# Strassen's scheme in the first projection and in the gate chunks of a two-block transformer kernel

## The reference, cut to what matters

```python
xn = rmsnorm(h, g_mix)                       # 256 x 2048
(q_a, k_c, v_c, k_s, v_s, k_w, v_w, g_nsa, c_q, c_kv, k_r,
 gate_a, gate_b) = jnp.split(xn @ w_in, bounds, axis=-1)
# q_a 1536 columns, then k_c, v_c, k_s, ... to k_r; gate_a and gate_b 2048 columns each
o_a = nsa_attention(...)                     # compressed, selected and window branches
o_b = mla_attention(...)
mixed = (sigmoid(gate_a) * (o_a @ w_o_nsa) + sigmoid(gate_b) * (o_b @ w_o_mla))
h = h + mixed @ w_out
```

## Time and profile before

| | |
|---|---|
| median of 3 runs | 2749.98 us (2749.94 to 2750.15) |
| the profiled execution: its time | 2749.45 us |
| its span | 2747.7 us |
| TensorE's mean granted clock | 0.998 |
| busy: TensorE, its weight loads, VectorE, ScalarE | 99%, 83%, 69%, 51% |
| matmuls | 12990 |
| HBM | 504.08 MB read, 184 GB/s |

### The profile page before, as it was taken

One profiled execution on the slowest core, in us unless ns is written; L12 is line 12 of the kernel. 1 busy time (PEld: TensorE's weight loads), 2 busy tenths in 40 slices (PEclk: granted clock), 3 DMA queues, 4 the chain that ended last, 5 costly groups with the idle time before them and its releaser, 6 DMA issues.

```text
span 2747.7 us, 30993 instructions
## 1 busy us (share of the span) xinstructions
PE 2732.1 (99%) x12990; PEld 2269.7 (83%) x12990; DVE 1882.3 (69%) x1699; ACT 1404.9 (51%) x1532; POOL 14.8 (1%) x28
## 2 busy tenths in 40 slices
PE   9999999999999999999999999999999999999999
PEld 7888778888888888888888888888788888888887
DVE  5445765455468878878788685665888489659765
ACT  5435663345566556455465545354554355445553
POOL 0000000000000000000000000000000000000000
PEclk9999999999999999999999999999999999999999
DMA  7645036555545555555555654545566555655555
GB/s 237 222 148 169 32 107 200 199 184 199 174 164 205 193 199 181 202 198 192 207 186 182 227 198 145 178 162 196 194 207 206 184 197 193 207 184 199 188 181 171
DMA packets 225082, 508.18 MB, mean 185 GB/s; under 512 B 9570, under 2 KB 20400, under 8 KB 224048
## 3 DMA queue, kind: packets, MB, share of 16 engines
q1 hardware_dynamic: 222752, 495.62, 52.8%
q0 software_dynamic: 2016, 10.36, 1.2%
q10 hardware_dynamic: 176, 0.23, 0.1%
HBM read 504.08 MB, written 2.10 MB: 184 GB/s over the span
## 4 chain that ended last, share of the span: by engine, by line
PE 86%; DVE 1%; ACT 1%; DMA 0%; issue 0%; ACTq 0%
PE acc L855 13%; PE acc L856 13%; PE acc L860 13%; PE acc L1338 7%; PE acc L1343 7%; PE acc L1339 7%; PE tb L1343 7%; PE tb L1338 7%; PE tb L1339 7%; PE tb L1328 1%; PE tb L840 1%; PE acc L1121 0%; PE tb L1172 0%; ACT prob L1908 0%; PE acc L1063 0%; PE acc L1060 0%
## 5 line engine op out<-in xcount | busy, mean ns | idle before, releaser
L2299 DVE TENSOR_TENSOR wlo<-raw,whi 128x2048 fp32r<-128x2048 f32 (+2 forms) x465 | 1023.7, 2212 | 565.8 <-ACT whi L1671 565.0
L1671 ACT ACTIVATE whi<-raw 128x2048 fp32r<-128x2048 f32 (+2 forms) x465 | 858.3, 1852 | 583.4 <-PE acc L860 317.4
L855 PE MATMUL acc<-whi,ahi 128*128 128x512 f32 (+1 forms) x1456 | 566.9, 390 | 0.4 <-DVE alo L2408 0.4
L856 PE MATMUL acc<-whi,alo 128*128 128x512 f32 (+1 forms) x1456 | 562.6, 387 | 0.0
L860 PE MATMUL acc<-wlo,ahi 128*128 128x512 f32 (+1 forms) x1456 | 357.6, 387 | 0.0
L855 PEld LDWEIGHTS acc<-whi,ahi 128*128 128x128 f32 x1456 | 274.3, 188 | 56.0 <-DVE wlo L2405 0.9
L856 PEld LDWEIGHTS acc<-whi,alo 128*128 128x128 f32 x1456 | 274.2, 188 | 54.5
L860 PEld LDWEIGHTS acc<-wlo,ahi 128*128 128x128 f32 x1456 | 271.0, 188 | 55.5
L1678 ACT ACTIVATE whi<-tsum 128x1024 fp32r<-128x1024 f32 x130 | 138.1, 1062 | 266.1 <-DVE tsum L2307 240.7
L1338 PE MATMUL acc<-whi,ff_hi 128*128 128x512 f32 x512 | 201.6, 394 | 0.2 <-DVE h L2371 0.2
L1339 PE MATMUL acc<-whi,ff_lo 128*128 128x512 f32 x512 | 199.7, 390 | 0.0
(11 more groups left out here) (408 smaller groups left out, 3650.5 us busy)
## 6 DMA issues: line engine op xcount, KB each, us to landing
raw<-in_w_ff SPq DMA_DIRECT2D x128, 1024.0 KB, 5.0
raw<-in_w_in SPq DMA_DIRECT2D x119, 1024.0 KB, 5.0
raw<-in_w_gate SPq DMA_DIRECT2D x88, 512.0 KB, 3.7
raw<-in_w_up SPq DMA_DIRECT2D x88, 512.0 KB, 4.6
raw<-in_w_down SPq DMA_DIRECT2D x44, 1024.0 KB, 5.1
raw<-in_w_out SPq DMA_DIRECT2D x16, 1024.0 KB, 5.1
raw<-in_w_o SPq DMA_DIRECT2D x16, 1024.0 KB, 5.1
raw<-in_w_ple_gate SPq DMA_DIRECT2D x16, 1024.0 KB, 5.2
```

The costliest lines, as they stand in the source:

```text
L855: nc.tensor.matmul(out_(t), hi[:, kt, tt(t)], whi[:, slot, wc(k)], start=first and k == 0, stop=False)
L856: nc.tensor.matmul(out_(t), lo[:, kt, tt(t)], whi[:, slot, wc(k)], start=False, stop=False)
L1671: nc.scalar.activation(whi[:, g % SPLIT, 0:n_], raw_of(n)[:, 0:n_], ACT.Copy).then_inc(w_hi, 1)
L2299: V.tensor_tensor(wlo[:, g % SPLIT, 0:n_], raw_of(load_of(g))[:, 0:n_], whi[:, g % SPLIT, 0:n_].bitcast(F32), ALU.subtract).then_inc(w_lo, 1)
```

## The change

Chunks 2 to 5 of the first projection become two double chunks (plan "DDSDSDSD"), and gate a and gate b of each column 1 to 3 become one double chunk with the same plan: five in all. They use differences in place of sums (kind N in place of T). The sums of the activation tiles, four tiles for each S step, are kept beside the activations, since D steps take the plain tiles: VectorE builds them (`tile_sums`: one operation on 128x512 and four on 128x128), ScalarE rounds (`sums_rounded`), VectorE subtracts (`tile_rests`). An eighth bank takes the last quadrant. VectorE folds the banks in five steps, and ScalarE scales or applies the sigmoid in place behind them.

```diff
+QKV_PLAN, GATE_PLAN = "DDSDSDSD", "DDSDSDSD"
...
-    plain(119)
+    plain(8)
+    for _ in range(2):
+        double(QKV_PLAN, (0, 1, 5), sums="N")
+    mark["qkv_end"] = len(kinds)
+    plain(8)
+    mark["narrow"] = len(kinds)
+    plain(2 + 4 + 3 + 2)
+    mark["fill"] = len(kinds)
+    plain(4 + 4)
+    for _ in range(3):
+        double(GATE_PLAN, (0, 1, 6), 2, sums="N")
+        mark["gates_end"] = len(kinds)
+        plain(4)
+    plain(16 + 4 + 4)
...
+        FIRST_LOAD = {2: G_XV + 4, 3: MARK["gud"] - 3, 4: MARK["gud"] - 3, 6: G_FILL + 5}
...
@@ GpSimd @@
-                pool.wait_ge(mm_done, 12)
+                pool.wait_ge(mm_done, MARK["qkv_end"])
...
-                pool.wait_ge(pv_done, items[calls[0][-1]]["u"] + 1)
+                pool.wait_ge(mm_done, MARK["gates_end"])
                 pool.dma_start(h[:, :, :], tok(a["x"])).then_inc(h_in, 16)
...
@@ TensorE @@
-            w.loop(2, lambda i: [chunk(ahi, alo) for _ in range(2)])
...
+            def summed_chunk(x, act_hi, act_lo, first_sums):
+                c, d = w.n["chunk"], w.n["double"]
+                x0, y0 = acc[c % 2], acc[(c + 1) % 2]
+                b2, q6, q3, q7 = x0[:, 0:COLS], x0[:, COLS:], y0[:, 0:COLS], y0[:, COLS:]
+                q5, q4, b1, q8 = tb[0][:, 0:COLS], tb[0][:, COLS:], tb[1][:, 0:COLS], tb[1][:, COLS:]
...
+                def direct(p):
+                    pe.wait_ge(w_hi, w.val("group", 1))
+                    parts = ((b2, 0, 0), (q3, 0, 1), (q4, 2, 0), (q8, 2, 1))
+                    if p == begin:
+                        pe.wait_ge(w_lo, w.val("group", 1))
+                    for n, (o, m, half) in enumerate(parts):
+                        if p == begin and n < 2:
+                            pe.wait_ge(acc_free[(c + n) % 2], (c + n) // 2)
+                        elif p == begin and d:
+                            pe.wait_ge(q_free, 2 * d + n - 3)
...
+                        if p == end and n < 3:
+                            mm.then_inc(bank_done, 1)
...
+            pe.wait_ge(small_ready, 5)
+            for _ in range(2):
+                summed_chunk(qkv_s, ahi, alo, 0)
             def cmp_turn():
+                summed_free()
...
             def gates(i, last=False):
-                chunk(ahi, alo)
-                chunk(bhi, blo, 8, hook=mixed_turn(0))
-                chunk(ahi, alo, hook=mixed_turn(1))
-                chunk(bhi, blo, 8, kt0=8, hook=mixed_turn(2))
+                summed_chunk(gate_s, ahi, alo, len(qkv_s.pairs))
+                chunk(bhi, blo, 8, hook={1: lambda: (summed_free(), mixed_turn(0))} if last else None)
+                chunk(bhi, blo, 8, kt0=8, hook={0: lambda: mixed_turn(1), 1: lambda: mixed_turn(2)} if last else None)
...
@@ ScalarE @@
+                block_of(items_[-1], hooks | {items_[-1] - 1: first_sum})
+                act.wait_ge(rstd_ready, NORMS.index(R_X) + 1)
+                for n in range(2):
+                    act.wait_ge(q_free, 2 * d + 1 + n)
+                    for t in range(TT):
+                        last = nc.scalar.activation(e[n][:, t, :], e[n][:, t, :], func, scale=rstd[:, R_X, t:t + 1])
+                    last.then_inc(by, 1)
...
@@ VectorE @@
+                def first_folds():
+                    dve.wait_ge(s1_out, d + 1)
+                    dve.wait_ge(bank_done, 3 * d + 1)
+                    V.tensor_tensor(e0, v2(x0[:, :]), both(e1[:, 0, :]), ALU.add).then_inc(free_x, 1)
+                    dve.wait_ge(free_x, c // 2 + 1)
+                    dve.wait_ge(bank_done, 3 * d + 2)
+                    V.tensor_tensor(e1, v2(y0[:, :]), both(e0[:, 1, :]), ALU.add).then_inc(free_y, 1)
+                block_of(items_, hooks | {items_ - 1: first_folds})
+                dve.wait_ge(free_y, (c + 1) // 2 + 1)
+                dve.wait_ge(bank_done, 3 * d + 3)
+                V.tensor_tensor(e0[:, 1, :], tb[0][:, COLS:2 * COLS], e1[:, 1, :], ALU.add).then_inc(q_free, 1)
+                dve.wait_ge(q_free, 2 * d + 1)
+                link(V.tensor_tensor(e1, both(tb[0][:, 0:COLS]), e1, ALU.add))
+                dve.wait_ge(mm_done, w.val("used"))
+                linked()
+                V.tensor_tensor(e1[:, 1, :], tb[1][:, COLS:2 * COLS], e1[:, 1, :], ALU.add).then_inc(q_free, 1)
...
             def kc_rope():
-                taken_by(dve, 3)
-                taken_by(dve, 4)
+                dve.wait_ge(qkv_ready, 3)
                 key_rope(O_KC, by=(cmp_in, 1))
...
+            block_of(2, {0: lambda: gate_sums(0), 1: lambda: (gate_rests(0), gate_sums(1))}, ev=first_mixed)
+            block_of(2, {0: lambda: (gate_rests(1), gate_sums(2)), 1: lambda: gate_rests(2)}, ev=first_second)
```

More of the change, by code:

```diff
@@ L142, in __init__ @@
     def __init__(self):
-        self.n = dict(group=0, chunk=0, turn=0, link=0, used=0, double=0, built=0, plain=0, ff=0, gud=0)
+        self.n = dict(group=0, chunk=0, turn=0, link=0, used=0, double=0, sums=0, built_x=0, built=0, plain=0, ff=0, gud=0)
     def val(self, name, off=0, div=1, mul=1):
@@ L216, in plain, with double @@
         ring.extend([slots] * n)
-    def double(plan, slots, dmas=1):
+    def double(plan, slots, dmas=1, sums="T"):
         for step in plan:
-            kinds.extend("BT" if step == "S" else "W")
+            kinds.extend("B" + sums if step == "S" else "W")
             loads.extend([dmas, 0] if step == "S" else [dmas])
             ring.extend([slots] * (2 if step == "S" else 1))
-    plain(119)
+    plain(8)
[12 more added lines that the diff above has]
+    plain(16 + 4 + 4)
+    mark["xv"] = len(kinds)
+    plain(4 + 4)
     mark["ff"] = len(kinds)
@@ L244 @@
 KINDS, LOADS, RING, MARK = item_kinds()
-SUMS_BEFORE = [KINDS[:g].count("T") for g in range(len(KINDS) + 1)]
-ITEM_OF = [g for g in range(len(KINDS)) if KINDS[g] != "T"]
-SLOTS = 5
+SUMS = "TN"
+SUMS_BEFORE = [sum(k in SUMS for k in KINDS[:g]) for g in range(len(KINDS) + 1)]
+ITEM_OF = [g for g in range(len(KINDS)) if KINDS[g] not in SUMS]
+SLOTS = 7
 def load_of(g):
-    return g - SUMS_BEFORE[g] - (KINDS[g] == "T")
+    return g - SUMS_BEFORE[g] - (KINDS[g] in SUMS)
 def load_slots():
@@ L269, with tile @@
 SLOT, BEFORE, LANDED = load_slots()
+@dataclass
+class Sums:
+    plan: str
+    hi: object
+    lo: object
+    rest: object
+    pairs: list
+    def tile(self, act, kept, pair, m, product):
+        if product and m > 2:
+            return kept[:, 4 * self.pairs.index(pair) + m - 3, :]
+        return act[:, 2 * pair + m % 2, m // 2 * P:(m // 2 + 1) * P]
 @dataclass
@@ L710, in _ @@
                     group(win, c * COLS, k * GKT)
-            w.loop(3, lambda i: [chunks(win, i * 2 * COLS + (j - 2) * COLS, 0) for j in range(2)], first=2)
+            for c in (2, 4):
+                for step in range(KT // 2):
+                    wide(win[:, 2 * step:2 * step + 2, c * COLS:(c + 2) * COLS])
+            for c in (6, 7):
+                chunks(win, c * COLS, 0)
             for k in (0, 2 * GKT):
@@ L721, in gates @@
             def gates(i):
-                at, at_a, at_b = i * COLS - COLS, i * COLS + (O_GA - COLS), i * COLS + (O_GB - COLS)
-                chunks(win, at_a, 0)
+                at = i * COLS - COLS
+                for step in range(KT // 2):
+                    load_pair(win, win, O_GA + at, step, O_GB + at)
                 chunks(wna, at, 0, 8)
-                chunks(win, at_b, 0)
                 chunks(wml, at, 0, 8)
@@ L2435, in _ @@
+            for n in range(2):
+                tile_sums(qkv_s, qkv_x[:, :, :], n)
+            for n in range(2):
+                tile_rests(qkv_s, n)
+            for c in (2, 4):
+                summed_chunk(qkv_s, (qkv[:, :, col(c)], qkv[:, :, col(c + 1)]),
+                             {5: lambda: tile_sums(qkv_s, qkv_x[:, :, :], 2), 6: lambda: tile_rests(qkv_s, 2)} if c == 2 else {})
             half = ROTA // 2
@@ L2677, in second @@
                     V.tensor_tensor(out_(), out_(), sgb[:, :, :], ALU.add).then_inc(done, 1)
[L2678 removed]
+                block_of(2, {0: lambda: mixed_turn(1), 1: lambda: mixed_turn(2)} if last else None, ev=second)
             conv(1)
```

178 lines of the change are left out of this document (138 added, 40 removed).

## The result

| | before | after |
|---|---|---|
| median | 2749.96 us (4 runs) | 2773.49 us (4 runs, 2771.78 to 2775.80) |
| ratio | | 1.0087, 95% interval 1.0075 to 1.0099 |
| the profiled execution, its span | 2749.45, 2747.7 us | 2772.40, 2770.6 us |
| mean granted clock | 0.998 | 0.994 |
| matmuls | 12990 | 12945 |

The change is slower by 23.5 us. The forecast was slower by 13.1 us, 2763, with a range that ended at 2773, half a microsecond under the median.

The account below looks back on a forecast made before the run. TensorE, 99% busy, was taken to bound the kernel, so each new wait lengthens it. Waits of +23.3 us against -10.2 for fewer matmuls gave +13.1, forecast 2763 us (chance 0.60), range 2750 to 2773.

Parts of the forecast that it names:

- The saving: Five double chunks: each takes 183 matmuls where two chunks took 192, 45 fewer in all, -10.2 us.
- The end of QKV: At chunk 6, item 30's load through item 29's slot delays the first fold: +4.5; +0.1 more between the QKV doubles.
- cmp_turn: TensorE waits for the rope on k, behind item 32's rest, its load issued beside w1k: +2.6 us (0.5 to 6).
- The first gate double: Entrance of the gates: item 57 late through item 56's slot, +3.3; then the late sum into mixed, +5.9 us.
- posT: Start of the first double: TensorE waits for the position copies, +1.2 us.
- mixed's transposes: After the last gate double the transposes wait for the last fold, +0.5 us.
- the second and third gate double: TensorE waits for the sum into mixed behind a late rest: +2.6 us each, +5.2 for two (2.8 to 9).
- rival D: New waits of 3 to 6 us lower TensorE's clock two to four times: +5 to +10, about 2770; chance 0.15.
- Rival B: Loads run further ahead, so both restart entrances cost nothing: -4.8, 2745 us; sign: item 29's rest by S+32.3; chance 0.08.
- A: Everywhere: all cover holds, so only the full gain of -10.2 remains, 2739.8 us; chance 0.04.
- C: The three entrances cost 7 in place of 16.3, the gate boundaries 2.8: +1.4, 2750 to 2755 us; chance 0.13.

Follow-up runs that it names:

- e1: Against the changed kernel: a ring that restarts no longer takes the slot of the load just before it; 2762.23 us (-11.3).
- e4: Against the changed kernel: the compressor's weights load when item 33 is done in place of item 29; 2776.05 us (+2.6).
- e2: Against the changed kernel: gate doubles' first step wants the bank awaiting the sum into mixed after 18 matmuls in place of 6; 2759.73 us (-13.8).
- e5: Against the changed kernel: VectorE does the sum into mixed ahead of the rest of the next double's second item; 2761.28 us (-12.2).
- e8: Six repairs: e7 plus, on ScalarE, the second scaling behind the first rounding that follows; 2741.07 us, ratio 0.9970 to the kernel before.
- e6: Changed kernel with four repairs: e1's ring, e2's bank order, w1k loaded after item 31, posT wait moved to the first S step; 2749.23 us, ratio 0.9996.
- e7_again: The kernel of e7, unchanged, run once more beside e8 and e9 on one chip; 2743.93 us, ratio 0.9981 to the kernel before.
- e9: Against e7: the compressor's weights load when item 29 is done again; 2743.91 us, ratio 0.9981 to the kernel before.
- e3: Against the changed kernel: TensorE does overwritten filler matmuls in the waits of the three gate doubles, no wait removed; 2769.52 us (-4.0).
- e7: Five repairs: e6's four plus e5's early sum into mixed; 2745.03 us, ratio 0.9982 to the kernel before.

## Why the prediction missed

Right, by its own steps:
- The saving: 45 matmuls, 12945 left. With six repairs 8.5 of the 10.2 us are there.
- The end of QKV: the series of rest, load, rounding, rest through one slot, and the fold behind it. 4.6 foreseen, 5.1 measured, and e1 took it away. Counted from S, the start of the second double (99.3), the rest of 29 ended at 35.9 for 35.5 and the bank was free at 46.6 for 45.9.
- cmp_turn: 2.6 foreseen, 2.0 measured. But I gave the load beside w1k as its cause. In the changed kernel that was so (without it, in e4, the wait is gone); with the ring mended ScalarE's scalings take its place, and the same 2.2 to 2.4 us stay. I had named the first and not seen the second waiting behind it.
- The first gate double: 9.2 foreseen, 8.4 measured, both mechanisms as described (e1 takes the first, e2 and e5 most of the second).
- posT 1.2 and mixed's transposes 0.5: 1.2 and 0.7.

A term too small: the second and third gate double, 2.6 each; 3.4 and 3.6 were measured, inside the ends given. The changed kernel at the second:

```profile
491.38 2.29 DVE L2454 TENSOR_TENSOR wlo<-raw,whi 128x2048 fp32r<-128x2048 f32 x1 [0.60 <-ACT whi L1801]
...
496.12 0.79 PE L1019 MATMUL acc<-whi,ahi 128*128 128x512 f32 x1 [3.24 <-DVE mixed L2893]
```

VectorE's rest of the second item ended at 493.67, 2.3 us after TensorE's start at 491.36, where I had 1.3. All waits together: 23.3 foreseen, 24.4 measured.

**The step that failed is the clock**, put down as rival D with a chance of 0.15 and left out of the sum. It belonged in it. Behind every wait of 3.2 us or more TensorE ran at half speed for a while, at all four places, 8.5 us in all, of which some 7 made the kernel longer. My argument against it was that "the whole span's mean clock is 0.998, so shorter waits did nothing". That is no evidence about waits of 3 to 6 us: the kernel before has none. Its longest single wait of TensorE is 1.5 us, and the one fall of the earlier trace rows was read as something of the compressor. The forecast and its rival were not alternatives: D follows from the forecast's own waits. Those of 4.5, 3.3 and 5.9 alone, at two places, give 2763 + 5 = 2768 at the text's own 2.6 a fall; with the second and third gate double, whose waits were foreseen at 2.6 and came to 3.4 and 3.6, it is 2763 + 10 = 2773. That this is so near the measured time is partly luck: a fall lost 2.1 us on average, not 2.6, and the waits were 1.1 longer. The range failed by the same step: its upper end left room for the falls or for a term above its middle, not for both. The high ends of the terms alone, +27 as the prediction adds them up, reach about 2777 and would have held the result; the range stopped at 2773 with no reason given.

Rival B, that the restarts would be covered, had a sign of its own, and the trace decides it: the rest of 29 ended at S+35.9 where S+32.3 was needed, and e1, which gives the loads a free slot, brought 11.3 us. A and C fell with it: the waits sum to 24.4.

Left open is part of what e8 still lacks to the full 10.2, 1.7 us by the medians and 1.1 by the spans of the profiled executions. Its profile shows 0.45 and 0.7 of wait and two small delays of 0.4 and 0.2 at the start of the second QKV double; against that, the clock's fall in the compressor part was shorter in it than in the kernel before and gave back about 1 us. In how many executions the clock falls behind cmp_turn no run tells.

## What to carry to other kernels

When a change makes a saturated TensorE wait, price the wait and then the lower clock behind it: here 1.4 to 3.0 us more for each wait of over 3 us with dense matmuls behind it, nothing for one of 1.2, and nothing where the slow matmuls lie ahead of another wait that ends at its own time. Where a ring of buffers changes its length, look whether two loads in a row fall into one slot; a line that skips the slot just used was worth 11 us. And where a scheme fills all eight PSUM banks, what decides at its ends is the order on the evicting engine: which operation frees the bank that is wanted first, and what stands ahead of it.

## What the runs showed of the hardware

The clock against the wait ahead of it, over the wait at chunk 6, at cmp_turn and at the gate doubles in all runs: behind waits of 0.9 to 2.0 us it never fell. Behind those of 2.2 to 2.7 us at cmp_turn it fell in three runs (e6 2.4, e7_again 2.2, e9 2.2) and not in four (e1 2.2, e3 2.7, e5 2.5, e7 2.4). Behind those of 3.2 us and more, 19 of them in the changed kernel and e1 to e5, it was always down, at the latest 1.2 us after TensorE had started again. The e2 run has one away from chunk 6 and the gates, a wait of 3.4 at cmp_turn:

```profile
161.99 1.32 PE L1101 MATMUL tb<-con,qkv 128*96 128x128 f32 x8 [3.37 <-DVE qkv L2543]
```

```profile
162.00:164.00 2.00, 2.00 (x13) 1.81 (x14) 2.00 (x1) 0.00 (x0) 0.00 (x0) 0.66 0.89 309
164.00:166.00 2.00, 2.00 (x8) 1.70 (x7) 0.06 (x1) 0.29 (x1) 0.00 (x0) 0.50 0.83 239
```

The time of an execution goes with it: the changed kernel's fastest, 2771.78 us, has a mean granted clock of 0.995, its slowest, 2775.80, has 0.993; e7's go from 2742.54 at 0.999 to 2748.07 at 0.997. Whether such waits widen the spread is not shown (e7's eleven executions lie 5.5 us apart, but e4's four, with the most waits, 1.8, and the kernel before's 23 beside e7 3.2). The fall in the compressor part, which every version has, lost 1.7 us in e1, e7 and e8, 3.4 in the kernel before and the changed one, and 6.8 in e4, by the granted clock in the 2 us stretches. Counted by the matmuls, e8 gained 1.1 us on the kernel before there, where the clock says 1.7. A term of one or two microseconds moves between kernels without any change at the place.
